# Four runs of unread products on TensorE between the last mix and the first experts

## The reference, cut to what matters

```python
y = jax.nn.gelu(y.reshape(nb, ns, SSM_WIDTH)).astype(x.dtype)
a = y @ w_out
out = a[..., :D_MODEL] * jax.nn.sigmoid(a[..., D_MODEL:])
xp = xp + mp                                    # residual, then hier_moe(rmsnorm(xp)):
pg = jax.nn.softmax((xt @ w_rg)); le = (xt @ w_re)   # group and expert logits
top_w, top_i = lax.top_k(pe, TOP_K)             # two experts of the chosen group
h = silu(xt @ w_gate) * (xt @ w_up)             # D_EXPERT = 256 wide
h = h * combine                                 # (t, e, f)
out = h @ w_down, summed over experts
```

## Time and profile before

| | us |
|---|---|
| median of 3 timed runs | 838.97 |
| lowest and highest of them | 836.39, 842.45 |
| profiled execution, its own time | 832.8 |
| its span, first to last instruction | 831.1 |

### The profile page before, as it was taken

How to read it: one execution, slowest core, us unless ns; L and a number is a source line. 1 busy time by engine, 2 the same in 40 slices (tenths; PEclk the granted TensorE clock), 3 DMA queues, 4 the chain that set the end, 5 groups by cost and what they waited for, 6 DMA issues and landing times.

```text
span 831.1 us, 15132 instructions
## 1 busy us (share of the span) xinstructions
PE 784.4 (94%) x4238; PEld 618.8 (74%) x4238; DVE 597.5 (72%) x1143; ACT 412.0 (50%) x770; POOL 318.7 (38%) x416
## 2 busy tenths in 40 slices
PE   7999989999999999998869999999999999999983
PEld 5888866655778778776747878888888888888762
DVE  7998789995534365457676788768687688678833
ACT  7557751125326353342353665666456666446621
POOL 3920011011000003205154576667666766666432
PEclk9999999999999999999989999999999999999996
DMA  8565316897734243333267587658676688686531
GB/s 308 171 219 181 112 30 230 191 153 220 291 107 151 78 151 115 115 127 104 102 229 286 185 309 259 225 173 277 246 265 219 197 299 307 220 313 219 197 103 78
DMA packets 57670, 161.27 MB, mean 194 GB/s; under 512 B 21856, under 2 KB 26464, under 8 KB 50912
## 3 DMA queue, kind: packets, MB, share of 16 engines
q1 hardware_dynamic: 34304, 112.99, 41.7%
q0 software_dynamic: 22976, 47.05, 16.2%
q10 hardware_dynamic: 288, 0.03, 0.0%
HBM read 129.07 MB, written 62.40 MB: 230 GB/s over the span
## 4 chain that ended last, share of the span: by engine, by line
PE 42%; DVE 4%; issue 3%; DVEq 1%; DMA 1%; ACT 0%; ACTq 0%; POOL 0%; POOLq 0%
PE pbig L1385 8%; PE pbig L1389 8%; PE pbig L1386 8%; PE pbig L1404 4%; PE pbig L1406 4%; PE pbig L1405 4%; PE pbig L1327 4%; PE pbig L1397 1%; DMA WR<-in_w_gu 1%; DVE WL L2004 1%; ACT WH L928 0%; PE pbig L1348 0%; DVE hh L1849 0%; PE pbig L1354 0%; DVEq L2114 0%
## 5 line engine op out<-in xcount | busy, mean ns | idle before, releaser
L1385 PE MATMUL pbig<-WH,xgH 128*128 (+1 forms) x304 | 122.9, 404 | 1.3 <-issue 1.1
L1386 PE MATMUL pbig<-WL,xgH 128*128 (+1 forms) x304 | 119.0, 391 | 0.0
L549 POOL DMA_INDIRECT records<-rec,at_rec x34 | 35.6, 1047 | 191.0 <-DVEq L1997 181.6
L1274 PE MATMUL pbig<-w2H,ysH 128*128 128x512 f32 x256 | 105.9, 414 | 0.0
L1275 PE MATMUL pbig<-w2L,ysH 128*128 128x512 f32 x256 | 101.3, 396 | 0.0
L1276 PE MATMUL pbig<-w2H,ysL 128*128 128x512 f32 x256 | 101.1, 395 | 0.0
L2004 DVE SCALAR_TENSOR_TENSOR WL<-WR,gf_p,WH 128x512 f32 (+1 forms) x128 | 86.2, 744 | 0.0
L928 ACT ACTIVATE WH<-WR,gf_p 128x512 f32 (+1 forms) x128 | 80.6, 712 | 2.6 <-issue 0.8
L1389 PE MATMUL pbig<-WH,xgL 128*128 (+1 forms) x304 | 77.0, 395 | 0.0
L623 POOL DMA_INDIRECT x_sums<-xg,recs x36 | 61.9, 1720 | 35.8 <-DVE xg L2108 20.6
L2108 DVE SCALAR_TENSOR_TENSOR xg<-pbig,recs,xg 128x1024 f32<-128x1024 f32 x39 | 49.9, 1280 | 28.8 <-PE pbig L1406 28.8
(11 more groups left out here) (354 smaller groups left out, 1734.5 us busy)
## 6 DMA issues: line engine op xcount, KB each, us to landing
WR<-in_w_gu SPq DMA_DIRECT2D x32, 1024.0 KB
WR<-in_w_dn SPq DMA_DIRECT2D x16, 1024.0 KB
xT<-in_x_cols SPq DMA_DIRECT2D x16, 512.0 KB, 3.6
low<-in_x_rows SPq DMA_DIRECT2D x16, 512.0 KB, 4.5
U<-in_x_rows SPq DMA_DIRECT2D x16, 512.0 KB, 5.2
x_mid<-x SPq DMA_DIRECT2D x16, 512.0 KB, 2.7
x_sums<-x SPq DMA_DIRECT2D x16, 512.0 KB, 3.9
w<-in_w_out SPq DMA_DIRECT2D x1, 4096.0 KB, 13.6
```

Source lines behind the costliest of these rows:

```text
L1274: pe.matmul(pbig[:, n, :], ysH[b][:, k, :], w2H[n][:, k, :], start=(k == 0), stop=False)
L1385: pe.matmul(pbig[:, 6, :], xgH[b][:, k, :], WH[:, ds(off + k * 2 * DE, 2 * DE)], start=(k == 0), stop=False)
L1386: pe.matmul(pbig[:, 6, :], xgH[b][:, k, :], WL[:, ds(low_ + k * 2 * DE, 2 * DE)], start=False, stop=False)
```

## The change

A new function `keep_busy(n, bank)` issues n products of 128x128 by 512 whose operands are weights that lie in `WH` anyway, each with its own weight load. They go to a PSUM bank whose content nobody reads before it is started anew. It waits only for the split of the first expert's weights. Four calls are put into TensorE's order: 8 after `e_turn(0, 0)`, 5 before `positions(3)`, 10 before `e_hturn(0, 0)`, and 4 before `up_second_hi(0, 4)`, 27 products in all. Nothing is removed or moved.

```diff
+            def keep_busy(n, bank):
+
+                pe.wait_ge(S["lo_split"], PIECES)
+                for _ in range(n):
+                    pe.matmul(pbig[:, bank, :], WH[:, EW:EW + P], WH[:, EW:EW + 512], start=True, stop=True)
+
             e_turn(0, 0)
+            keep_busy(8, 5)
             up_first(0, 4)
             c_turn(TF)
             up_first(4, 10)
             c_logit(TF)
             c_fold(TF)
             up_first(10, 3 * KD)
+            keep_busy(5, 1)
             positions(3)
             pe.matmul(pbig[:, 4, 0:NE], ones[:, :], EE[:, TF, :], start=True, stop=False)
             pe.matmul(pbig[:, 4, 0:NE], ones[:, :], EP[:, TF, :], start=False, stop=True).then_inc(S["tot_done"], 1)
             pe.nop().then_inc(S["dn_done"], 1)
             second_turn(0)
+            keep_busy(10, 1)
             e_hturn(0, 0)
             second_turn(1)
+            keep_busy(4, 1)
             up_second_hi(0, KD // 2)
```

## The result

| | before | changed |
|---|---|---|
| median of 6 runs | 838.88 us | 832.24 us |
| lowest, highest | 836.39, 842.45 | 830.68, 833.54 |
| span of the profiled execution | 831.1 us | 829.7 us |

The medians are 6.6 us or 0.8% apart. The ratio on record is 0.9933, with a 95% interval of 0.991 to 0.9955, which is 5.6 us, between 3.8 and 7.5. Between the two profiled executions there are only 1.4 us. Both facts need an explanation, and they have different ones.

A forecast was written before the change was run, and what follows sets the result against it. The loop was taken as bound by TensorE, so only its start could move: 0.36 + 0.24 + 1.23 - 0.2 = 1.65 us, rounded 1.7; 838.97 - 1.7 = 837.3 us. Range 833.5 to 841.5 us.

The forecast's parts named there:

- The clock's fall: TensorE's clock falls at 428.12 and returns at 438.36, 10.24 us at 1.2 GHz; the fillers should keep it full.
- more than that: Rival: timed executions spend longer at half clock in these gaps; another third of 10.24 us saves 1.7 us: 835.6, chance 0.10.
- The term: Gain from full clock through the end of `e_down(0)`, slid forward to `e_up(2)`: together 1.85 us.
- Steps 1 to 6: From 428 to `e_up(2)`: `up_second_hi` gains 0.36 us, words 0.6, `e_down(0)` 1.23; later products slide forward whole.
- Step 7: `e_turn(3)` waits for slot 3's gather, landing near 451.2: 0.2 us lost, bounds 0 and 1.8.
- Step 8: The stall at 487, with a weight DMA of 6.72 us, hangs on TensorE's progress and slides forward too.
- the third rival: Clock holds, but the gain is given back to the gather or at the stall ahead of 487: 838.9, chance 0.15.
- the slower rival: Clock falls at the same place and fillers run at half clock: +1.4 to +2.6 us, 841.0 in the middle, chance 0.10.
- the fall at 431 to 435: Rival: clock holds longer, then falls there; `e_down` pays 2.4 us, about 0 to 0.8 lost: 839.3, chance 0.15.
- The class "within 1%": Measured time within about 1% (8.4 us) of before, chance 0.93; faster 0.04, slower 0.03.

The follow-up runs named there:

- b_again: The kernel before, timed and profiled again unchanged: 836.88 us against 836.69 us for before in the same series.
- all_fold: The changed kernel plus seven more fillers ahead of the fold of the last tile: 833.89 us against 836.69 us for before.
- nop54b: The kernel before plus 54 empty instructions and no fillers, in the fourth series: 827.54 us against 831.60 us for before.
- all_stallb: The changed kernel plus nine small products in the wait ahead of slot 6, fourth series: 824.69 us against 831.60 us for before.

## Why the prediction was wrong

**The step that failed is one that was not there.** The sum priced 27 products, the clock and the waits, and ended at the start of the loop; it took for granted that added instructions leave everything else where it was. They moved TensorE's later code by 54 instructions, and with a shift of 54 a hole of about 2 us in the tail is gone, whether fillers or empty instructions make it. The prediction read the tail only for its clock. Just ahead of the row that it quotes stand 2.03 us of "issue" between `hh` and its transpose, and it did not ask what they were. Alone, this part was timed at 2.4 and 4.1 us (ratios 0.9977 and 0.995, both intervals below 1), of which the hole is 2.1. With it and the 1.7 us the forecast would have been near 833 to 835.

**Carrying the profile over to the median.** Of the 6.2 us between the profiled execution and the median, most seem to lie ahead of the change: the profile of b_again is 4.2 us longer than the first, and arrives at `e_turn(0)` 4.1 us later. Carrying them over was right for the difference, as far as the luck lay ahead of everything that changes. The half clock of this execution in the region, 10.2 us, was not lucky: the six profiles without fillers have 10.8 in the mean.

**The clock's fall, in place and size: right, on the low side.** The rival "more than that", by which timed executions spend longer at half clock, had a chance of 0.10. It is not what happened: it asked for a third more than 10.24 us there. All six profiles without fillers here have 6.8 to 13.7 us at half clock, and the ten with all four have none. The term was 1.85 us up to `e_up(2)`, 1.62 in the profiled pair, 2.6 over the means. (The prediction's own sum, 0.36 + 0.24 + 1.23 - 0.2, is 1.63 and not 1.65; it changes nothing.) The clock part alone was timed at 1.6 and 3.2 us. The first is just what was forecast, but its interval reaches up to no change.

**Steps 1 to 6: right.** `up_second_hi` stayed behind ScalarE. The words start with a wait of 0.58 us and take about 0.54 us where I took 0.7. `e_down(0)` takes 2.9 us, up to 437.63, against 2.79 forecast and 4.02 before.

**Step 7: right in kind, too small.** The wait on the gather is there, 1.59 us in the first profile of the change and 0.34 in all_fold. I took 0.2, with 1.8 as the far bound. GpSimd's last write of the table starts 24.4 us after `e_turn(0)` in both profiles, so it did not move with TensorE, as said; only the DMAs behind it landed sooner.

**Step 8: wrong.** I said that the stall ahead of 487 slides forward whole. In the first profile of the change it grew by 1.0 us, and the clock fell behind it. Among the seven profiles with all four runs of fillers and none ahead of slot 6, it fell there in four; among the eight with fewer or no fillers in one (nop54b); in the three with fillers ahead of slot 6 in none. That is the third rival, gain given back, with a chance of 0.15. It was real: 1.5 us in the means of the profiles, where the forecast had 0.2. How much of it the fillers ahead of slot 6 win back is not settled, 2.3 us by medians and 0.5 by means in all_stallb. Why the weight DMA takes 7.63 us and not 6.72 was not tried.

**The other rivals.** The clock never fell in this region with all four runs, so neither the slower rival nor the fall at 431 to 435 occurred in ten profiles. The class "within 1%" came out, at 0.93.

What stays open: the first six runs gave 6.6 us between the medians (5.6 by the ratio), the later series 3.0 and 4.6 (by means 3.9 and 5.6). The intervals overlap, and the runs do not say more than that the change is worth 3 to 7 us. The profiles account for 3.2 of them; whatever is above that is not explained.

## What to carry to other kernels

Short runs of unread products in TensorE's waits are worth their price when what follows is bound by TensorE; look at each later wait too, since a wait that was harmless may now be the one in which the clock falls. Adding or removing instructions ahead of a branch moves the code behind it, and empty instructions alone were worth 2.4 and 4.1 us here: time the change beside a kernel with as many empty instructions. A profiled execution that lies below all timed runs should be split at a point ahead of the change before anything is carried over to the median.

## What the runs showed of the hardware

TensorE stood still for 1.85 us between the weight load of a transpose and its product, behind a branch, while it waited for nothing that the profile shows. The hole was there with the code moved by 0 and by 256 instructions, and gone with 26, 28, 54, 68, 90 and 108. It ended 1.4 to 1.5 us after a packet of 16 KB of the instruction queue, in all five profiles that have it. Thirty small products put into that wait took 3.6 to 3.9 us where `hh` was ready after 1.9, and in one of two profiles such a hole cut them apart for 1.65 us more.

Runs of up to 20 float32 transposes of a constant, put between products, kept the clock at 2.4 GHz as half as many products of 128x128 by 512 did (granted clock 1.00 from 412 to 450 in both).

In executions of the same kernel the half-clock stretches stand in different places: 394, 428 and 810 in one of before, 50, 398, 435 and 814 in the other. Half-clock time between 412 and 450 ranged from 6.8 to 13.7 us over six executions without fillers: one execution of each kernel is too few to price the clock.
